# Recurrent gates' products in 64x64 blocks over the four quarters of the array

## What is computed

```python
LRU_WIDTH = (3 * MIX_WIDTH) // 8          # 384
LRU_HEADS = 6                             # six blocks of 64x64
    xh = xf.reshape(B, L, LRU_HEADS, LRU_HEAD_DIM)
    r = jax.nn.sigmoid(jnp.einsum('blhi,hij->blhj', xh, w_a) + b_a).reshape(B, L, W)
    i = jax.nn.sigmoid(jnp.einsum('blhi,hij->blhj', xh, w_x) + b_x).reshape(B, L, W)
    log_a = LRU_C * r * jax.nn.log_sigmoid(lam.astype(jnp.float32))
    a = jnp.exp(log_a)
    mult = jnp.sqrt(-jnp.expm1(2.0 * log_a))
    bterm = mult * i * xf
```

## Time and profile before

| | us |
|---|---|
| median of 3 runs | 1203.65 (1203.19 to 1204.58) |
| the profiled execution | 1207.14 |
| its span on the core | 1205.3 |
| PE busy in the span | 1153.6 |
| ACT busy | 428.2 |
| DVE busy | 704.6 |
| mean granted clock of PE | 0.978 |

### The profile page before, as it was taken

One profiled execution on the slowest core, in us unless ns is written; L12 is line 12 of the kernel. 1 busy time (PEld: TensorE's weight loads), 2 busy tenths in 40 slices (PEclk: granted clock), 3 DMA queues, 4 the chain that ended last, 5 costly groups with the idle time before them and its releaser, 6 DMA issues.

```text
span 1205.3 us, 19527 instructions
## 1 busy us (share of the span) xinstructions
PE 1153.6 (96%) x7381; PEld 1104.5 (92%) x7381; DVE 704.6 (58%) x1253; ACT 428.2 (36%) x716; POOL 305.3 (25%) x263
## 2 busy tenths in 40 slices
PE   4899999989989999999999999999999999999997
PEld 1698888888978999899999999999999999999996
DVE  5561355577875434777755655655655745656646
ACT  5552354545445343641331320421411311412431
POOL 0441101110525267762120120210210210210352
PEclk9699999999988999999999999999999999999998
DMA  8813434656333822111120121121120211111104
GB/s 307 305 62 110 106 108 137 209 173 197 115 107 106 264 71 72 52 54 36 51 72 23 49 70 36 38 68 34 52 70 17 66 56 32 55 52 36 35 1 141
DMA packets 61702, 109.87 MB, mean 91 GB/s; under 512 B 6434, under 2 KB 30278, under 8 KB 61254
## 3 DMA queue, kind: packets, MB, share of 16 engines
q1 hardware_dynamic: 51430, 84.88, 21.7%
q10 hardware_dynamic: 10208, 24.12, 6.4%
HBM read 96.81 MB, written 12.18 MB: 90 GB/s over the span
## 4 chain that ended last, share of the span: by engine, by line
PE 65%; DVE 2%; ACT 2%; issue 1%; POOL 1%; POOLq 0%; ACTq 0%; DVEq 0%
PE D L2296 13%; PE D L2298 13%; PE D L2297 13%; PE X L2298 5%; PE X L2296 5%; PE X L2297 5%; PE D L2112 3%; PE D L2114 3%; PE D L2113 3%; POOL H_lo L975 0%; DVE X L1556 0%; DVE B L1542 0%; DVE FU L1871 0%; ACT Y_hi L1268 0%; DVE FU L1684 0%
## 5 line engine op out<-in xcount | busy, mean ns | idle before, releaser
L975 POOL TENSOR_TENSOR Y_lo<-FU,Y_hi 128x344 fp32r<-128x344 f32 (+2 forms) x120 | 123.2, 1031 | 560.5 <-ACT Y_hi L1115 554.2
L1831 DVE SCALAR_TENSOR_TENSOR X<-D,MOD,X 128x344 f32<-128x344 f32 (+1 forms) x216 | 123.8, 573 | 136.3 <-PE D L2298 113.8
L2296 PE MATMUL D<-Y_hi,W_hi 128*128 128x344 f32 x576 | 185.2, 322 | 0.0
L2298 PE MATMUL D<-Y_hi,W_lo 128*128 128x344 f32 x576 | 184.1, 320 | 0.0
L2297 PE MATMUL D<-Y_lo,W_hi 128*128 128x344 f32 x576 | 184.1, 320 | 0.0
L2112 PE MATMUL D<-H_hi,W_hi 128*128 128x344 f32 x472 | 160.2, 339 | 3.7 <-POOL H_lo L975 3.1
L2113 PE MATMUL D<-H_lo,W_hi 128*128 128x344 f32 x472 | 153.5, 325 | 0.0
L2114 PE MATMUL D<-H_hi,W_lo 128*128 128x344 f32 x472 | 153.2, 325 | 0.0
L2296 PEld LDWEIGHTS D<-Y_hi,W_hi 128*128 128x128 f32 x576 | 108.5, 188 | 1.2 <-issue 0.9
L970 POOL TENSOR_TENSOR W_lo<-RAWW,W_hi 128x1024 fp32r<-128x1024 f32 x25 | 61.6, 2462 | 186.1 <-ACT W_hi L1110 185.7
L2298 PEld LDWEIGHTS D<-Y_hi,W_lo 128*128 128x128 f32 x576 | 108.5, 188 | 0.0
(11 more groups left out here) (358 smaller groups left out, 2670.8 us busy)
## 6 DMA issues: line engine op xcount, KB each, us to landing
RAWW<-in_W SPq DMA_DIRECT2D x76, 512.0 KB, 3.6
RAWW<-in_WADA ACTq DMA_DIRECT2D x28, 512.0 KB, 4.2
RAWW<-in_WADA SPq DMA_DIRECT2D x20, 512.0 KB, 8.0
RAWW<-in_W ACTq DMA_DIRECT2D x18, 512.0 KB, 4.2
X0T<-in_x SPq DMA_DIRECT2D x3, 1376.0 KB, 12.7
out_y<-OUTN SPq DMA_DIRECT2D x24, 172.0 KB
X<-in_x SPq DMA_DIRECT2D x8, 344.0 KB, 4.6
NM<-nm_d SPq DMA_DIRECT2D x8, 256.0 KB, 5.9
```

The lines of the kernel that those rows point to most:

```text
L975: nc.gpsimd.tensor_tensor(lo_v, fu_v, hi_v.bitcast(F32), ALU.subtract).then_inc(lo_ready, 1)
L1831: tell(V.scalar_tensor_tensor(out=tile(X, m_x, a, a + w), in0=DB[bank][:, 0:w], scalar=tile(MOD, m_g, 0, 1), in1=tile(X, m_x, a, a + w), o ...
L2296: T.matmul(out, w_h, hi(kt), start=(kt == 0), stop=False)
L2298: one = T.matmul(out, w_l, hi(kt), start=False, stop=(kt == n - 1))
```

## The change

The six 128x128 products of `LRUG` become twelve of 64x64, without the zeros. For each chunk PE issues four: the two heads of the first gate from the array's upper left and lower right quarter into the two halves of one bank, and the two heads of the second gate from the other two quarters into another bank, so that the second gate's heads stand in the opposite half of the partitions. The four of a chunk share no wait; before the first of them PE waits for both banks. The banks go round in the order (X0, X1), (X2, X0), (X1, X2).

ACT now goes by chunk: it waits for the chunk's last product, makes the first gate in one instruction and the second in two of 64 partitions, each of which crosses to the other half on its way to `IG`. Their bias must lie in the half that is read, so a small tile `BX` holds it with the halves exchanged, filled by two more DMAs of SP behind that of `BDL`; `ld_bdl` is waited for at 48 on PE and, newly, on ACT.

```diff
@@ -219,9 +219,9 @@
             for w in range(2):
                 add(("TS", w), ("X3", "X4")[w])
         elif k == "LRUG":
-            for g in range(2):
-                for c in range(NCH):
-                    add((*s, g, c), ("X0", "X1", "X2")[c])
+            for c in range(NCH):
+                for g in range(2):
+                    add((*s, g, c), ("X0", "X1", "X2")[(2 * c + g) % 3])
         elif k == "S":
             add(("S", s[1]), "X0")
             add(("KT", s[1]), "X3")
@@ -400,6 +400,7 @@
         ADS, SEL = at("ADS", [P, 2 * P], rSB), new("SEL", [P, DEC + 1])
         COLS, IDN, ONE = new("COLS", [P, NCOLS]), new("IDN", [P, P]), new("ONE", [P, P])
         RT = new("RT", [P, 2, NCH, 3])
+        BX = new("BX", [P, LRU_T])
         EPT, LS = new("EPT", [P, 1]), new("LS", [P, 6, LRU_T])
         OUTC = new("OUTC", [P, LRU_T, CONV - 1])
         OUTL = new("OUTL", [P, LRU_T, DEC + 1])
@@ -737,6 +738,9 @@
                 elif k == "G1":
                     sp.wait_ge(full_ready, P_NORM)
                     sp.dma_start(BDL[:], I["bdl"]).then_inc(ld_bdl, 16)
+                    k = _COLS["bx"][0]
+                    for h in range(2):
+                        sp.dma_start(BX[64 * h:64 * h + 64, :], I["cols"][64 - 64 * h:128 - 64 * h, k:k + LRU_T]).then_inc(ld_bdl, 16)
                 elif k == "G3":
                     sp.wait_ge(nm_ready, 1)
                     sp.dma_start(nm_d, GR[:, R_NM, :]).then_inc(nm_stored, 16)
@@ -1208,14 +1212,18 @@
                         hi_key(s)
                 elif k == "LRUG":
                     t = s[1]
-                    for g, (dst, bias) in enumerate(((RG, "ba"), (IG, "bx"))):
-                        for c in range(NCH):
-                            key = (*s, g, c)
-                            wait_full(act, key)
-                            nc.scalar.activation(dst[:, c * CH:(c + 1) * CH], bank(key)[:, 0:CH], ACT.Sigmoid,
-                                                 bias=col(bias, t)).then_inc(free(key), 1)
+                    act.wait_ge(ld_bdl, 48)
                     for c in range(NCH):
-                        b, n = use[(*s, 1, c)]
+                        at = slice(c * CH, (c + 1) * CH)
+                        key = (*s, 1, c)
+                        wait_full(act, key)
+                        nc.scalar.activation(RG[:, at], bank((*s, 0, c))[:, 0:CH], ACT.Sigmoid,
+                                             bias=col("ba", t)).then_inc(free((*s, 0, c)), 1)
+                        nc.scalar.activation(IG[0:P // 2, at], bank(key)[P // 2:P, 0:CH], ACT.Sigmoid, bias=BX[P // 2:P, t:t + 1])
+                        nc.scalar.activation(IG[P // 2:P, at], bank(key)[0:P // 2, 0:CH], ACT.Sigmoid,
+                                             bias=BX[0:P // 2, t:t + 1]).then_inc(free(key), 1)
+                    for key in ((*s, 1, 1), (*s, 0, 2), (*s, 1, 2)):
+                        b, n = use[key]
                         act.wait_ge(x_free[b], n + 1)
                 elif k == "LRUA":
                     t = s[1]
@@ -2180,11 +2188,15 @@
                 elif k == "LRUG":
                     t = s[1]
                     pe.wait_ge(xc_ready, t + 1)
-                    pe.wait_ge(ld_bdl, 16)
-                    for g in range(2):
-                        for c in range(NCH):
-                            key = (*s, g, c)
-                            done(T.matmul(take(key)[:, 0:CH], BDL[:, g * LRU_T + t, :], XC[:, c * CH:(c + 1) * CH], start=True, stop=True), key)
+                    pe.wait_ge(ld_bdl, 48)
+                    H = P // 2
+                    for c in range(NCH):
+                        at = slice(c * CH, (c + 1) * CH)
+                        r, x = take((*s, 0, c)), take((*s, 1, c))
+                        T.matmul(r[0:H, 0:CH], BDL[0:H, t, 0:H], XC[0:H, at], start=True, stop=True)
+                        T.matmul(x[0:H, 0:CH], BDL[H:P, LRU_T + t, H:P], XC[H:P, at], start=True, stop=True)
+                        done(T.matmul(r[H:P, 0:CH], BDL[H:P, t, H:P], XC[H:P, at], start=True, stop=True), (*s, 0, c))
+                        done(T.matmul(x[H:P, 0:CH], BDL[0:H, LRU_T + t, 0:H], XC[0:H, at], start=True, stop=True), (*s, 1, c))
                 elif k == "TS":
                     for kind in ("k", "q"):
                         d, n = dense_use(unit_of(kind, ML_T - 1), NCH - 1)
```

## The result

The changed kernel takes 1213.8 us (median of 4 runs, 1211.75 to 1215.6) against 1203.42 of the kernel before on the same chip (4 runs, 1202.95 to 1204.58): the ratio is 1.0088, with a 95% interval of 1.0070 to 1.0107. It is 10.4 us slower. The forecast was slower, at 1211.0; the time lies inside its range (1206 to 1215) and 0.3 above the likeliest case's own range.

The account below looks back on a forecast made before the run. PE, busy 96% of the span, was taken as the bound. Lost PE time of 2.8 us in the gate stages plus 4.5 of low clock made +7.3, a median of 1211.0 us, range 1206 to 1215.

Parts of the forecast that it names:

- likeliest case: Whole kernel: quarters overlap fully and the low clock comes; 1211.0 us, own range 1208.5 to 1213.5, chance 0.57.
- The products: PE in LRUG: a group of four overlapping quarters takes 0.73 us, three 2.2, against 3.7 us a tile before.
- rival of partial overlap: Gate groups on PE: quarters go in pairs, 1.35 us a group, +12.9, 1216.5; chance 0.12 together with no overlap.
- The table load: ACT in LRUG: the sigmoid's table load falls behind the first group, at 0.89 us, first sigmoid at 2.18.
- rival in which it stays ahead: ACT in LRUG: table load still made ahead of the product, stages 4.1 to 4.6 us, +1.0, 1204.7; chance 0.08.
- The stage waits: PE in the three LRUG stages: idles for banks, stages become 5.00 us; +1.16, +0.91 and +0.75, together +2.8 us.
- three in a row start 0.44 apart: ACT's sigmoids of one chunk: three take 1.42 us, so ACT is free at 3.50, before the second group at 3.67.
- The chain over DVE: ACT's later gates delay LRUA, DVE and XC: +2.1 us at tile 1's first product, covered if PE is later.
- The clock: Behind each of three LRUG stages PE falls to 1.2 GHz for 3.3 us, 1.5 us lost each, +4.5 together.
- rival without a low clock: PE's clock stays up in the gates, DVE's +2.1 decides at tile 1: +3.8, 1207.5; chance 0.18.
- The rest: Waits for ld_bdl cost nothing; nothing of the loss is taken up later, bounds 0 to 1.5 us.
- From the trace to the median: Profiled execution forecast at 1214.4; it lies 3.5 us above the median of 1203.65, so the median comes to 1211.0.

Follow-up runs that it names:

- e5: Changed kernel with filler matmuls in both waits of each LRUG and eight more ahead of tile 1's first product; 1211.57 us, ratio 1.0079.
- e1: Changed kernel without ACT's wait for ld_bdl in LRUG, so that the table load comes ahead again; 1212.72 us, ratio 1.0075.
- e2: Changed kernel with 12 and 4 filler matmuls, adding nothing to the output, in the two waits of each LRUG; 1210.41 us, ratio 1.0054.
- e4: Changed kernel without ACT's ld_bdl wait, with 9 and 6 matmuls of the next dense product put between the gate groups; 1206.39 us, ratio 1.0022.
- e3: Kernel before, whole 128x128 products, with one ACT wait added that puts the table load behind the first product; 1205.38 us, ratio 1.0018.
- e7: Kernel before with the gates of tiles 1 and 2 moved later in the order of steps; 1203.71 us, ratio 1.0015.
- e9: Kernel before with small matmuls, results overwritten, ahead of PE's long waits between 220 and 400 us; 1206.4 us, ratio 1.0037.

## Why the prediction was right, and where it was off

**The products**: right. A group was put at 0.73 us by the strips of the earlier trace rows; in e5 tile 1's first record is at 176.04 and the next matmul at 176.78, 0.74. The rival of partial overlap fell with it, though each group has an upper and a lower row quarter writing into one bank. The page of the Trainium skill that was cited with that rival ("PSUM — Partial Sum Buffer", PSUM bank collisions) says that different row tiles can't access one bank at the same time, but what it has measured of this are writes into one bank and one quadrant of the partitions. Here the two writers of a bank stand in different quadrants, and the rows above show no delay. The estimate from the packing rule of the Trainium skill ("TensorE: Matmul & The Clock Gate", Part 3) was 0.1 us a group too short: 0.63 against 0.74.

**The table load**: right in place and size. It was forecast at 0.9 us after the first record and came at 0.95; the first sigmoid at 2.18, came at 2.24. The rival in which it stays ahead fell, and its price was wrong as well: it was put at +1.0 without a low clock, and e1, which brings that case about, stands 9 us above before because the clock falls there too.

**The stage waits**: right mechanism, too small. 2.8 us was the sum, 4.14 was measured (e5, at the full clock). A little of that is how the stages were read: 4.09 and 4.25 end 0.16 us ahead of the second dense record, and behind the quarters that record comes 0.26 after the first one, so 0.1 us a tile was left out in tiles 1 and 2. In the rest three links failed by little each. The group is seen at 0.95, not 0.89. PE's second group starts 0.70 after the sigmoid (150.56 to 151.26), not 0.60. And "three in a row start 0.44 apart" was read from whole gates; with half sigmoids the starts are 0.58, 0.55 and 0.57 apart. All instructions of one line, and two first gates of tile 1:

```profile
L1222 ACT ACTIVATE IG<-X,BX x9: 544/545/546, 151.1 to 217.2; 64x344 f32<-64x344 f32 x9
```

```profile
180.14 0.55 ACT L1220 ACTIVATE RG<-X,COLS 128x344 f32<-128x344 f32 x1
...
181.84 0.55 ACT L1220 ACTIVATE RG<-X,COLS 128x344 f32<-128x344 f32 x1
```

So ACT itself held up the second chunk: its first sigmoid started 1.70 us after that of the first chunk in tiles 1 and 2 (2.04 in tile 0, whose second group ran at the low clock already) where 1.49 was reckoned, and the third group came at 4.63 at the earliest, not 4.27.

**The chain over DVE**: right to be there and to be covered. It was +2.1 and measured +2.93 in e2 (ACT ends tile 2's gates at 7.30 after the first product, not 6.58). In after PE was later, and no wait for `XC` shows; where the clock was mended, it came up at once (e2, e4).

**The clock**: right in kind, 1 us short. Three stretches of 3.3 us were expected, +4.5; there were three, but tile 0's was 6.8 us long, 13.7 us in all and 5.44 us of time. The rival without a low clock fell: it would be e5's state, which the fillers had to bring about, at +5.65 in the first part and not +3.8. The reason that the prediction gave, PE busy for a smaller share than in a row that preceded a low clock, does not hold alone: in e4 PE stands from 172.93 to 175.60, and the clock stays at 1.00. The remark that four quarters at once might count as full work was not put to a test, as PE is idle for half of the stage.

**The rest**: nothing is seen to be taken up later, as forecast. No wait of PE or ACT in the stages is for the data of `BX` or `BDL`; what ACT's wait for `ld_bdl` costs, it costs by where it puts the table load (e1).

**From the trace to the median**: the step was sound, the agreement of the traces was luck. Taking 3.5 us off is the same as adding the cost to the median of before, and 1203.42 + 9.6 = 1213.0 lies 0.8 below the measured 1213.8. On its own traces the sum looks almost perfect, 1214.4 forecast and 1214.21 measured, but by two errors against each other: the gates cost 9.6 instead of 7.3, and the second part came out 2.4 shorter, by its low clock of 17.1 instead of 23.9 us. Of the error of 2.8 us, 2.3 are the gates' under-sizing (1.3 in the waits, 1.0 in the clock); the medians' 10.4 less 9.6, some 0.8, is within what the second part scatters, and 0.2 goes the other way, since before's median came down by that much with its fourth run.

**Open**: the second part costs the changed kernel nothing beyond its low clock, but whether the change shifts how much of that there is, two traces of each kernel can't tell (10.2 and 23.9 us before, 17.1 and 17.1 after). Why e5's median (+8.7) lies so far above its trace's first part (+5.65) is open in the main; its untraced runs had the lower mean clock. Elsewhere ratio and first part go together: +10.6 and +9.6 us in after, 9.0 and 9.5 in e1, 2.2 and 1.9 in e3, 2.6 and 0.9 in e4, 1.8 and 1.65 in e7. And the spread of all versions, 6 us between runs, remains with the clock up (e9), so low clock isn't all of it. No version ran faster than the kernel before.

## What to carry to other kernels

Packing small matmuls pays only if the partner that empties the banks keeps up: look at how many products can be issued before the first bank must come back, and don't put that return behind a partner's table load. Where PE is the bound, idle gaps can cost twice, once as waiting and once as low clock behind it, as those of 2.12 us did in every stage here; a single gap of 2.67 us didn't (e4), so look at the granted clock and not at the gap. Filling the gaps with work that is needed anyway took the ratio from 1.0075 (e1) to 1.0022 (e4); filling waits for other engines further on with empty work made the kernel slower (e9). Compare two kernels part by part, cut at the same products, set the low clock of each part beside its length, and trace each kernel twice before a difference of less than 6 us is put down to an edit.

## What the runs showed of the hardware

- Two products from different row halves of the array wrote two halves of one bank at the same time, and two others a second bank, and none waited for another: starts within 0.02 us, second passes 0.34 us later. The group was done for PE in 0.74 us, against 0.62 for one whole product.
- A sigmoid on 64 partitions takes 541 to 546 ns (547 to 548 on 128, all of 344 columns) and starts 0.55 to 0.58 us after the one before, although its bank was full; whole ones of the first gate start 0.44 apart. That crossing to the other half or the array's quarters cause this was not tried.
- Stages with one wait of 0.82 us kept the full clock (e3). Those with a wait of 2.12 us and one of 0.76 or 0.89 us lost it in all six cases of two traces; in tile 0 it fell behind the first wait already, at 151.47. A low clock followed one wait of 1.42 us (e2) and none followed one of 2.67 us (e4). Taking 0.94, 0.58 and 0.50 us off the first waits (e1) went with a longer low clock, 17.1 against 13.7 us, in the one trace taken.
- In ten traces the second part, some 2000 records of PE in each, took 316.85 to 324.25 us, in step with 10.2 to 27.3 us at the low clock.
